# Where the light expert blocks' ScalarE and VectorE work stands among the weight splits of a decoder trunk

## What is computed

```python
logits = xf @ router
top_logits, top_idx = lax.top_k(logits, 2)
gates = jax.nn.softmax(top_logits, axis=-1)
# for each expert e, with the rows xb of the tokens that chose it:
y = (jax.nn.silu(xb @ w_gate[e]) * (xb @ w_up[e])) @ w_down[e]
# out[token] = sum over its two experts of gate * y
```

## Time and profile before

| | us |
|---|---|
| median of 3 runs | 1610.12 |
| the profiled execution | 1610.06 |
| its span | 1608.3 |
| TensorE busy (matmul) | 1488.0 (93%) |
| VectorE busy | 907.0 (56%) |
| ScalarE busy | 730.8 (45%) |
| GpSimd busy | 313.9 (20%) |

### The profile page before, as it was taken

How to read it: one execution, slowest core, us unless ns; L and a number is a source line. 1 busy time by engine, 2 the same in 40 slices (tenths; PEclk the granted TensorE clock), 3 DMA queues, 4 the chain that set the end, 5 groups by cost and what they waited for, 6 DMA issues and landing times.

```text
span 1608.3 us, 22560 instructions
## 1 busy us (share of the span) xinstructions
PE 1488.0 (93%) x9592; PEld 1135.9 (71%) x9592; DVE 907.0 (56%) x678; ACT 730.8 (45%) x613; POOL 313.9 (20%) x295
## 2 busy tenths in 40 slices
PE   9999999999999999998988888899888998898885
PEld 8888799999988787886655565566555665565554
DVE  5555567555658668885444454435444544455445
ACT  5443454343454357774443344334443443344443
POOL 5599317100056009900000000000000000000001
PEclk9999999999999999999999999999999999999998
DMA  9644567855501659999998999999899999999994
GB/s 349 180 161 156 184 194 273 294 184 184 183 27 34 224 188 378 395 386 353 376 359 333 354 388 347 348 344 392 337 354 345 392 375 354 359 394 350 347 352 153
DMA packets 202269, 469.61 MB, mean 292 GB/s; under 512 B 7880, under 2 KB 20384, under 8 KB 202160
## 3 DMA queue, kind: packets, MB, share of 16 engines
q1 hardware_dynamic: 198096, 454.57, 77.2%
q0 software_dynamic: 3920, 13.44, 2.6%
q10 hardware_dynamic: 144, 0.07, 0.0%
HBM read 462.02 MB, written 15.21 MB: 297 GB/s over the span
## 4 chain that ended last, share of the span: by engine, by line
PE 69%; DMA 16%; DVE 5%; ACT 5%; issue 4%; POOL 1%; POOLq 0%; SPq 0%; DVEq 0%; ACTq 0%
PE PS L2013 66%; DMA weights_raw<-in_moe_w_up 8%; ACT weights_hi L1054 4%; DMA weights_raw<-in_moe_w_down 4%; DMA weights_raw<-in_moe_w_gate 3%; DVE weights_lo L1494 2%; PE PS L2142 1%; PE PS L2255 1%; POOL b_padded L874 1%; PE PS L2414 0%; ACT c_padded L1054 0%; DMA results_by_slot<-small_expert_rows 0%; DVE small_act_rows L1494 0%; DMA row_back<-results_by_slot,pair_index 0%; PE PS L2583 0%
## 5 line engine op out<-in xcount | busy, mean ns | idle before, releaser
L1494 DVE TENSOR_TENSOR weights_lo<-weights_raw,weights_hi 128x2048 fp32r<-128x2048 f32 (+1 forms) x293 | 677.1, 2312 | 575.5 <-ACT weights_hi L1054 573.3
L1054 ACT ACTIVATE weights_hi<-weights_raw 128x2048 fp32r<-128x2048 f32 (+1 forms) x293 | 559.0, 1909 | 672.1 <-PE PS L2013 226.8
L2013 PE MATMUL PS<-weights_hi,gathered_hi 128*128 128x512 f32 x560 | 227.5, 406 | 21.1 <-DVE weights_lo L1494 18.8
L2013 PE MATMUL PS<-weights_hi,gathered_lo 128*128 128x512 f32 x560 | 222.6, 398 | 0.0
L2013 PE MATMUL PS<-weights_lo,gathered_hi 128*128 128x512 f32 x560 | 221.5, 395 | 0.0
L2013 PE MATMUL PS<-weights_hi,act_transposed_hi 128*128 128x512 f32 x456 | 187.3, 411 | 4.6 <-DVE weights_lo L1494 4.6
L2013 PE MATMUL PS<-x_transposed_hi,weights_hi 128*128 128x256 f32 x640 | 180.8, 283 | 1.2 <-DVE weights_lo L1494 1.0
L2013 PE MATMUL PS<-weights_hi,act_transposed_lo 128*128 128x512 f32 x456 | 180.3, 395 | 0.0
L2013 PE MATMUL PS<-weights_lo,act_transposed_hi 128*128 128x512 f32 x456 | 179.7, 394 | 0.0
L2013 PE MATMUL PS<-x_transposed_hi,weights_lo 128*128 128x256 f32 x640 | 179.5, 280 | 0.0
L2013 PE MATMUL PS<-x_transposed_lo,weights_hi 128*128 128x256 f32 x640 | 179.4, 280 | 0.0
(11 more groups left out here) (326 smaller groups left out, 1474.5 us busy)
## 6 DMA issues: line engine op xcount, KB each, us to landing
weights_raw<-in_moe_w_up SPq DMA_DIRECT2D x111, 1024.0 KB, 10.1
weights_raw<-in_moe_w_down SPq DMA_DIRECT2D x111, 1024.0 KB, 9.9
weights_raw<-in_moe_w_gate SPq DMA_DIRECT2D x110, 1024.0 KB, 10.1
weights_raw<-in_ret_w_in SPq DMA_DIRECT2D x24, 1024.0 KB, 6.7
weights_raw<-in_ffn_w_gate SPq DMA_DIRECT2D x14, 1024.0 KB, 5.1
weights_raw<-in_ffn_w_up SPq DMA_DIRECT2D x14, 1024.0 KB, 5.1
weights_raw<-in_ffn_w_down SPq DMA_DIRECT2D x14, 1024.0 KB, 5.0
weights_raw<-in_ret_w_out SPq DMA_DIRECT2D x8, 1024.0 KB, 5.0
```

The source lines that it names most:

```text
L1054: return nc.scalar.activation(o, i, ACT.Copy)
L1494: return nc.vector.tensor_tensor(o, a, b, op)
L2013: return nc.tensor.matmul(o, l, r, start=start, stop=stop)
```

## The change

In both lists, the work of light block k moves from odd l = 2k + 5 to even l = 2k + 4: it now stands ahead of the split of the first unit of heavy block k + 2, and so one split earlier than before. Within one l the order stays: `expert_work`, `after_small`, split. The two copies of the first light expert's rows (l = 4 and 6) stay where they are. Nothing is computed otherwise, and TensorE, GpSimd and SyncE keep their lists.

```diff
@@ first_pass of ScalarE @@
                             if l in (2 * LAG, 2 * LAG + 2):
                                 gather_small(LIGHT[0], l // 2 - LAG)
-                            j = small_after((l - 5) // 2) if l % 2 else None
+                            j = small_after((l - 4) // 2) if l % 2 == 0 else None
                             if j is not None:
                                 after_small(j)
```

## The result

The changed kernel takes 1541.32 us (median of 4 runs, 1540.33 to 1542.10) against 1610.55 us before (4 runs): a ratio of 0.9575, 95% interval 0.9558 to 0.9592, so 69.2 us less. Its profiled execution took 1541.29 us, span 1539.5.

A forecast was written before the change was run, and what follows sets the result against it. Bound by transfers, with a hole at each TensorE wait for a light product. Stage 832 to 758 us saves 74, less 5 for hiccups, plus 1.3 at the end: 70, rounded to 68, so 1610 - 68 = 1542 us; range 1526 to 1576.

The forecast's parts named there:

- The cause: Alternating stage: TensorE loses 65.1 us in 15 light transposes waiting for VectorE's product, which stands behind a split awaiting its transfer.
- The time with full transfers: Alternating stage: at 394 GB/s, the rate of four stretches without such a wait, 832 us become 758.
- the sum: Whole kernel: 74 us from the stage, less 5 for hiccups, plus 1.3 at the end, 70, rounded down to 68.
- The 5 us taken off for hiccups: Stage: four remaining transfer losses of 1.35 us each kept, at changes of expert, 5 us in all.
- the upper bound: Whole kernel at 390 GB/s with twice the dips: 1610 - 66 - 10 + 1, given as 1555 us.
- rival C: Stage: no change, as the mean rate is a true limit or something else holds the product; 1605 to 1610 us, chance 0.05.
- The example: One light up block: product done at 858.0, transpose wanted at 860.1, so its wait goes with 2.1 us to spare.
- New waits ahead of the splits: ScalarE waits for TensorE's light block ahead of unit 2k+4's split; cost 0, at most 4.8 us for each of 63 blocks.
- rival D: ScalarE's new wait holds splits and buffer release: slower from 1.2 us per light block, 1662 us at 2; chance 0.03.
- What is late next: TensorE in the stage: idle 46 us against 96, in waits of about 1 us for split weights.
- the tail: End of the kernel: last light block's output copy runs at about 1563.6, right behind its products, 1.3 us gained.
- Rival B: Stage: late weight units bring 2.4-us standstills at half clock, taking half the gain; 1560 to 1600 us, chance 0.17.

The follow-up runs named there:

- kernel 1: Only VectorE's product moved one split earlier, ScalarE's light work left as in the kernel before: 1544.82 us, ratio 0.9593 to the kernel before.
- kernel 2: Only ScalarE's light work moved one split earlier, VectorE's product left as in the kernel before: 1609.57 us, ratio 0.9992 to the kernel before.
- kernel 6: Changed kernel with the light work one split further ahead in both lists, ahead of unit 2k+3: 1544.23 us, ratio 0.9568 to the kernel before.
- Kernel 7: Changed kernel with the light work two splits further ahead in both lists, ahead of unit 2k+2: 1746.71 us, ratio 1.0833 to the kernel before.
- Kernels 4 and 5: Kernel before the change with half, then seven eighths, of each light unit's transfer left out: 1528.36 us, then 1524.25 us.

## Why the prediction was right

- **The cause.** A product of 0.42 us hung on a transfer through one split in VectorE's list. Kernels 1 and 2 confirm it from both sides: 66 us with VectorE's move alone, none with ScalarE's alone.
- **The time with full transfers.** 394 GB/s was read from stretches without a wait; 392 came. From 736 us to the end of the last light products the changed kernel takes 756.4 us (to 1492.4) against 827.5 (to 1563.5): 71.1 us less, where the sum had 74 - 5 = 69. The 5 us taken off for hiccups came as a rate 2 GB/s short, which is 4 us. The sum has two slips: the four full stretches weighted by length give 394.6 GB/s, so 757 us and not 758, and the upper bound is 1610 - (66 - 10 + 1) = 1553, not 1555. Neither moves the forecast.
- **The Trainium skill's 358 GB/s** (DMA: Bandwidth & Descriptors, Where 436 GB/s comes from) is passed by 34 GB/s over 764 us on this core working alone; rival C falls with it.
- **The example.** 2.1 us between product and transpose forecast, 2.2 measured.
- **New waits ahead of the splits, taken as 0.** They cost nothing that can be seen at the place chosen: the rate is 392 GB/s, and in kernel 6 one split further ahead costs at most 3 us. Kernel 7 shows that it is a matter of place, as rival D said; its price, 205 us over 63 blocks or 3.3 us each, was above the 2 us used there.
- **What is late next.** Waits for weights 48.7 us against "some 45"; light down products 3.65 us each against 3.7. TensorE's idle time came out at 56 us in place of 46, in a stage 6 us longer than the 758 of the estimate.
- **The step that failed: the tail.** I gave it 1.3 us; it lost 2.3 (from the last light products to the end of the span 47.1 us against 44.8). The last output copy does stand one split earlier, but another split and a heavy copy, both ahead of it in ScalarE's list, ran late; that split waited for its transfer. ScalarE after the change:

```profile
1492.09 1.91 ACT L1054 ACTIVATE weights_hi<-weights_raw 128x2048 fp32r<-128x2048 f32 x1 [0.80 <-DMA weights_raw<-in_moe_w_gate]
1493.91 0.58 ACT L1054 ACTIVATE act_transposed_hi<-PS 128x512 fp32r<-128x512 f32 x1
1494.38 0.59 ACT L1054 ACTIVATE small_expert_rows<-PS 128x512 f32<-128x512 f32 x1
```

The products end at 1492.4, the copy starts at 1494.38: 2.0 us behind them, against 1.4 before, and not the 0.1 I had forecast. The larger part of the loss comes behind the copy. From its start to that of the additions it is 23.6 us (1494.38 to 1517.97) against 21.5 (1564.93 to 1586.45), and GpSimd issued its four row fetches over 8.5 us, from the start of the first to that of the last, in place of 6.3. That interval runs from 6.3 to 8.6 us in the profiles of this case whichever the order (7.9 in kernel 2, 6.6 in kernel 1), so its cause stays open. All told the stage gave 2.1 us more than its terms and the tail 3.6 less; with the sum of 70 rounded down to 68 this ends at 1541.32 against 1542. The mechanism gave the 70; that the forecast is off by less than 1 us is luck, as errors of either sign cancelled.

- **Rival B** came in one place of the stage and not in a row of them. Of 48 waits for weights the longest is 2.70 us; the clock falls to 0.68 behind it, but the transfers go on. The clock of the stage is 1.00, and the lowest of its 4-us stretches (736:740, 740:744 and so on) moves 329 GB/s:

```profile
772.02 0.47 PE L2013 MATMUL PS<-weights_hi,gathered_hi 128*128 128x512 f32 x1 [2.70 <-DVE weights_lo L1494]
772.00:776.00 4.00, 3.98 (x12) 3.20 (x13) 3.72 (x3) 2.65 (x3) 0.00 (x0) 0.68 1.03 410
788.00:792.00 4.00, 4.00 (x18) 2.47 (x15) 2.85 (x2) 0.68 (x2) 0.00 (x0) 1.00 1.01 329
```

- **What the prediction left out.** It named the full queue as the reason why the unit is late. Kernels 4 and 5 show that with fewer bytes half of each wait would have stayed. The forecast did not rest on it, but whoever had taken from it "move fewer bytes" would have got 83 us and kept 15 waits.

## What to carry to other kernels

In an engine's list, a short instruction that the critical engine needs soon must not stand behind one that waits for a transfer; look for small products whose releaser in the chain is a weight load. Judge a stage's transfer limit by stretches without such a wait, not by its mean, and move the instruction only as far ahead as the work behind it has cover: here one split was worth 69 us, a second nothing that can be told from noise, a third cost 200.

## What the runs showed of the hardware

- Where transfers bind, new short waits of TensorE need not add to the time in full: 13.1 us in five pieces of 2.0 to 4.0 us in kernel 1 went with 3.5 us of time, while the waits for weights were 11.9 us less. The 65.1 us in 15 pieces of 3.4 to 5.3 us in the kernel before went with 66, with the half-clock pieces and the empty DMA engines behind them.
- The clock does not follow the length of a wait alone: in kernel 1 it stood at 0.57 in the 4 us behind a wait of 2.0 us (at 992) and at 1.00 behind one of 2.1 us (at 1290).
- Eight times smaller light loads did not bring whole 1 MB units down in proportion: from about 10 us to landing with full loads (medians) to some 7 with half and 6.0 to 7.2 with an eighth.
